# Two-layer GLA and short-conv encoder: attention stage cut into 512-token segments whose steps stand between projections

## The reference

```
q, k, v, r, gl = split(x @ w_in)             # 512 | 512 | 1024 | 1024 | 16
log_a = log_sigmoid(gl @ w_gate_up + b) / 16 # 512
cum = cumsum(log_a) inside each chunk of 64 tokens; tot = its last row
k_dec = k * exp(tot - cum)
S_c = exp(tot) * S_{c-1} + k_dec^T v         # per head, 128 x 256, 4 heads, 32 chunks
o = q @ S_c                                  # every token of chunk c reads the state after c
o = rmsnorm_per_head(o) * gn * silu(r)
x = x + o @ w_out
```

## Time and profile before

| | us |
|---|---|
| median of 3 runs | 1712.02 (1711.77 to 1791.83) |
| the profiled execution, device time | 1712.97 |
| its span on the slowest core (core 1) | 1711.7 |
| spans of the 8 cores | 1707.7 to 1711.7 |
| mean granted PE clock, all cores | 0.940 to 0.943 |

### The profile page before, as it was taken

How to read it: one execution, slowest core, us unless ns; L and a number is a source line. 1 busy time by engine, 2 the same in 40 slices (tenths; PEclk the granted TensorE clock), 3 DMA queues, 4 the chain that set the end, 5 groups by cost and what they waited for, 6 DMA issues and landing times.

```text
span 1711.7 us, 20982 instructions; the slowest of 8 cores (1707.7 to 1711.7 us)
## 1 busy us (share of the span) xinstructions
PE 1520.2 (89%) x7440; PEld 709.7 (41%) x7440; DVE 830.8 (49%) x1078; ACT 715.8 (42%) x1163; POOL 81.3 (5%) x123
## 2 busy tenths in 40 slices
PE   3996656995556699999999999999999999999998
PEld 1443223542223344444444454444544444444443
DVE  3013553105644455355545665556655544554557
ACT  5424435425446542044034564333654404412445
POOL 0010000010000000000000000000001000000000
PEclk9997677996777899999999999999999999999999
DMA  9562001561020033012322324333033202232204
GB/s 249 77 92 32 1 1 38 76 98 25 1 35 16 13 50 49 13 26 43 50 37 44 38 25 57 43 49 40 13 50 49 35 16 38 44 50 38 42 15 184
DMA packets 67557, 80.80 MB, mean 47 GB/s; under 512 B 4591, under 2 KB 54016, under 8 KB 67456
## 3 DMA queue, kind: packets, MB, share of 16 engines
q0 software_dynamic: 61840, 59.86, 25.5%
q1 hardware_dynamic: 5616, 19.62, 3.3%
HBM read 130.93 MB, written 8.39 MB: 81 GB/s over the span
## 4 chain that ended last, share of the span: by engine, by line
PE 83%; ACT 6%; DVE 5%; issue 3%; DMA 2%; DVEq 0%; ACTq 0%; POOL 0%; POOLq 0%; SPq 0%
PE PS L425 34%; PE PS L372 26%; PE PS L504 10%; PE PS L668 3%; PE PS L685 3%; DMA wring<-a_w_in 2%; PE PS L607 2%; PE PS L637 2%; DVE gl_ot_u L770 2%; ACT xtm L308 2%; DVE gl_s_u L730 1%; DVE gl_of_u L773 1%; PE PS L340 1%; ACT xn_shared_u L260 1%; PE PS L642 1%
## 5 line engine op out<-in xcount | busy, mean ns | idle before, releaser
L425 PE MATMUL PS<-xn_shared_u,wring 128*128 128x512 bf16 x2816 | 614.8, 381 | 5.1 <-ACT xn_shared_u L260 3.9
L425 PEld LDWEIGHTS PS<-xn_shared_u,wring 128*128 128x128 bf16 x2816 | 276.4, 98 | 340.0 <-issue 12.6
L372 PE MATMUL PS<-wring,ffn_h_u 128*128 128x512 bf16 x1408 | 306.8, 379 | 0.0
L379 DVE TENSOR_TENSOR X<-X,PS 128x512 f32<-128x512 f32 x256 | 174.2, 687 | 215.1 <-PE PS L372 212.6
L437 ACT ACTIVATE ffn_a_u<-PS,vecs_sb 128x1024 f32<-128x1024 f32 x88 | 98.1, 1114 | 274.3 <-PE PS L425 274.3
L372 PEld LDWEIGHTS PS<-wring,ffn_h_u 128*128 128x128 bf16 x1408 | 137.3, 98 | 163.3
L451 ACT ACTIVATE ffn_a_u<-ffn_a_u 128x1024 f32<-128x1024 f32 x88 | 93.0, 1057 | 228.3 <-DVE ffn_a_u L449 228.3
L504 PE MATMUL PS<-xn_shared_u,wring 128*128 128x512 bf16 x768 | 166.2, 379 | 1.2 <-ACT xn_shared_u L260 1.2
L452 DVE TENSOR_TENSOR ffn_h_u<-ffn_a_u,PS 128x1024 bf16<-128x1024 f32 x88 | 107.4, 1221 | 123.0 <-ACT ffn_a_u L451 117.7
L447 DVE SCALAR_TENSOR_TENSOR ffn_a_u<-ffn_g_u,vecs_sb,ffn_a_u 128x1024 f32<-128x1024 f32 x88 | 113.0, 1284 | 77.8 <-ACT ffn_g_u L445 73.2
L449 DVE SCALAR_TENSOR_TENSOR ffn_a_u<-ffn_g_u,vecs_sb,ffn_a_u 128x1024 f32<-128x1024 f32 x88 | 113.0, 1284 | 9.2
(11 more groups left out here) (83 smaller groups left out, 1092.8 us busy)
## 6 DMA issues: line engine op xcount, KB each, us to landing
wring<-f_w_up POOLq DMA_DIRECT2D x16, 1024.0 KB, 12.2
wring<-a_w_in POOLq DMA_DIRECT2D x12, 1024.0 KB, 14.4
wring<-f_w_down POOLq DMA_DIRECT2D x44, 256.0 KB, 9.5
X<-x SPq DMA_DIRECT2D x16, 512.0 KB, 15.8
out<-X SPq DMA_DIRECT2D x16, 512.0 KB, 2.7
wring<-f_w_up POOLq DMA_DIRECT2D x8, 768.0 KB, 12.0
wring<-b_w_in POOLq DMA_DIRECT2D x12, 512.0 KB, 10.3
wring<-a_w_out POOLq DMA_DIRECT2D x16, 256.0 KB, 6.9
```

The source lines that it names most:

```text
L372: ins = nc.tensor.matmul(self.PS[:, b, :], Y[:, k, yi * 128:(yi + 1) * 128], w[k].ap[:, n * 512:(n + 1) * 512], start=(k == 0), stop=(k == ...
L379: lambda: nc.vector.tensor_tensor(xs, xs, self.PS[:, b, :], ALU.add))
L425: ins = nc.tensor.matmul(self.PS[:, bank0 + t, :], w.ap[:, kc, jb * 128:(jb + 1) * 128], XN[:, kc, (hh * 2 + t) * 512:(hh * 2 + t + 1) * 512],
```

## The change

The attention stage has no halves and no barriers. After `gla_start` it is a loop over four segments of 512 tokens: `gla_project(sg)` (gate, q, r) and `gla_scan(sg)` (tile by tile k and v). The six weight blocks of `w_in` and `w_out` have places of their own in one arena (`at`, with `inherit` taking over the waits of what lay there before) and are loaded once. `w_out` comes as f32 by SP into the places of X tiles 8 to 15, DVE multiplies gn into it (`late_wo`) and writes bf16 `Wo`, and only then SP loads x tiles 8 to 15 (`late_x`). SP issues x tiles 0 to 3 first and waits for `Wk` before w_out and x tiles 4 to 7.

The scan works on tiles of two chunks. `g_update(g, hp)` makes two heads of both chunks in banks 4 and 5, `g_read(g)` writes both chunks' o into banks 6 and 7, where it stays: ACT squares it from there, `g_gated` multiplies it there by the rstd and then by silu(r). All other groups rotate over banks 0 to 3. Update, read-out, statistics, gating and output projection of tiles g-1 and g-2 stand between the projections of tile g; those of the segment's last tiles stand in the next `gla_project`, and after the last segment in the list `left`, which `ffn(0)` now pumps between its first matmuls together with the norms of tiles 8 to 15. Tiles 0 to 7 are normed for the FFN in the last segment's scan. The first four units (`hh` = 0) have banks 0 to 3 alone for their pairs.

`ffn`, `sconv` and the rest keep their operations; H, Y and XN are two tensors of 1024 tokens each.

```diff
-NXTM = 4
+NXTM = 3
...
-        self.gla()
-        with ExitStack() as eso:
...
+        self.gla_start()
+        for sg in range(T // SEG):
+            self.gla_project(sg)
+            self.gla_scan(sg)
+        left = self.gla_end()
+        self.load_gamma("b_norm")
+        self.ffn(0, left, lambda i: self.norm_tile("b_norm", i))
...
+    def gla_start(self):
...
+        for i in range(4):
+            self.sp.dma(self.X[:, i, :], xv[i], [], self.bX[i])
+            if i == 0:
+                self.load_gamma("a_norm")
+                self.sp.dma(self.consts[:], self.consts_d, [], [self.bconst])
+                self.sp.dma(self.vecs[:], self.vecs_d, [], [self.bconst])
...
+        self.pool.dma(self.WGU[0:17, :], self.a_wgu, [], [self.bWGU])
+        self.pool.dma(self.Wg[:], win[:, :, 3072:3088], [], [self.bWg])
+        self.pool.wait(self.bX[2][0].w)
+        self.pool.dma(self.Wq[:], win[:, :, 0:512], [], self.bWq)
+        for h in range(2):
+            self.pool.dma(self.Wr[:, h], win[:, :, 2048 + h * 512:2560 + h * 512], [], [self.bWr[h]])
+        self.pool.dma(self.Wk[:], win[:, :, 512:1024], [], self.bWk)
+        for h in range(2):
+            self.pool.dma(self.Wv[:, h], win[:, :, 1024 + h * 512:1536 + h * 512], [], [self.bWv[h]])
+        self.sp.wait(self.bWk[0].w)
+        for k in range(KC):
+            self.sp.dma(self.X[:, 8 + k, :], wout[k], [], self.bX[8 + k])
+        for i in range(4, 8):
+            self.sp.dma(self.X[:, i, :], xv[i], [], self.bX[i])
+        self.late_wo = [lambda k=k: self.dve.op(
+            self.bX[8 + k] + [self.bconst], [self.bWo[k]], lambda: nc.vector.tensor_scalar(
+                self.Wo[:, k, :], self.X[:, 8 + k, :], self.vcol("a_gn", k), None, ALU.mult))
+            for k in range(KC)]
+        self.late_x = lambda: [self.sp.dma(self.X[:, i, :], xv[i], [], self.bX[i]) for i in range(8, NTT)]
+        self.wo = [WBlock(self.Wo[:, k, :], [self.bWo[k]], None) for k in range(KC)]
+        self.singles = (0, 1, 2, 3)
+        for i in range(4):
+            self.norm_tile("a_norm", i)
+            self.turn(1)
+        self.turn()
...
+    def g_update(self, g, hp):
+        nc = self.nc
+        s = g % 2
+        def mmu():
+            ins = None
+            for h in (2 * hp, 2 * hp + 1):
+                for c in range(2):
+                    p = slice(c * 64, c * 64 + 64)
+                    ins = nc.tensor.matmul(self.PS[:, 4 + c, (h % 2) * 256:(h % 2 + 1) * 256],
+                                           self.KD[p, s, h * 128:(h + 1) * 128],
+                                           self.V[p, s, h * 256:(h + 1) * 256], start=True, stop=True)
+            return ins
+        self.pe.op([self.bKD[s], self.bV[s * 2 + hp]], [self.bPS[4], self.bPS[5]], mmu)
+        for c in range(2):
+            for h in (2 * hp, 2 * hp + 1):
+                self.dve.op([self.bS[(1 - c) * HEADS + h], self.bDEC[g], self.bPS[4 + c]], [self.bS[c * HEADS + h]],
+                            lambda: nc.vector.scalar_tensor_tensor(
+                                self.S[:, c, h, :], self.S[:, 1 - c, h, :], self.DEC[:, h, 2 * g + c:2 * g + c + 1],
+                                self.PS[:, 4 + c, (h % 2) * 256:(h % 2 + 1) * 256], ALU.mult, ALU.add))
+            hs = slice(2 * hp, 2 * hp + 2)
+            self.copy_on(self.act, self.SB[:, c, hs, :], self.S[:, c, hs, :],
+                         self.bS[c * HEADS + 2 * hp:c * HEADS + 2 * hp + 2], [self.bSB[c * 2 + hp]])
+    def g_read(self, g):
+        nc = self.nc
+        q = g // 4 % 2
+        i = g % 4
+        for c in range(2):
+            def mmo():
+                ins = None
+                for j in range(KC):
+                    h, hv = j // 2, j % 2
+                    ins = nc.tensor.matmul(self.PS[:, 6 + c, j * 64:(j + 1) * 64],
+                                           self.SB[:, c, h, hv * 128:(hv + 1) * 128],
+                                           self.QT[:, q, h, i * 128 + c * 64:i * 128 + c * 64 + 64], start=True, stop=True)
+                return ins
+            self.pe.op(self.bSB[c * 2:c * 2 + 2] + self.bQT[q * HEADS:(q + 1) * HEADS], [self.bPS[6 + c]], mmo)
+        self.act.op([self.bPS[6], self.bPS[7]], [self.bOF[g % 2]], lambda: nc.scalar.activation(
+            self.OF[:, g % 2].rearrange("p j (c t) -> p c j t", c=2),
+            self.PS[:, 6:8, :].rearrange("p c (j t) -> p c j t", t=64), AF.Square))
+    def g_stats(self, g):
+        nc = self.nc
+        b = self.bank()
+        osq = self.OF[:, g % 2].rearrange("p (h v) t -> p v h t", v=2)
+        def mmn():
+            nc.tensor.matmul(self.PS[:, b, :], self.onesV[:], osq[:, 0], start=True, stop=False)
+            return nc.tensor.matmul(self.PS[:, b, :], self.onesV[:], osq[:, 1], start=False, stop=True)
+        self.pe.op([self.bOF[g % 2], self.bconst], [self.bPS[b]], mmn)
+        self.rstd_from_psum(self.RS[:].rearrange("p h t -> p (h t)"), self.PS[:, b, :], [self.bPS[b]], self.bRS)
+    def g_gated(self, g):
+        nc = self.nc
+        i = g % 4
+        for c in range(2):
+            o = self.PS[:, 6 + c, :].rearrange("p (h v t) -> p h v t", h=HEADS, v=2)
+            rs = self.RS[:, :, c * 64:(c + 1) * 64].unsqueeze(2).broadcast_to([128, HEADS, 2, 64])
+            self.dve.op([self.bRS, self.bPS[6 + c]], [self.bPS[6 + c]], lambda: nc.vector.tensor_tensor(o, o, rs, ALU.mult))
+        self.dve.op([self.bPS[6], self.bPS[7]] + self.bSR, [self.bOF[g % 2]], lambda: nc.vector.tensor_tensor(
+            self.OF[:, g % 2].rearrange("p j (c t) -> p c j t", c=2),
+            self.PS[:, 6:8, :].rearrange("p c (j t) -> p c j t", t=64),
+            self.SR[:, :, i * 128:(i + 1) * 128].rearrange("p j (c t) -> p c j t", c=2), ALU.mult))
+    def gla_project(self, sg):
+        g = 4 * sg - 1
+        tail = g >= 0
+        norm = sg >= 1 and sg < 3
+        n0 = 4 * sg + 4
+        self.g_gate(sg)
+        if tail:
+            self.g_stats(g - 1)
+            self.g_update(g, 0)
+        if norm:
+            self.norm_tile("a_norm", n0)
+        self.g_softplus(4 * sg)
+        self.g_q(sg, 0)
+        if tail:
+            self.g_gated(g - 1)
+            self.g_update(g, 1)
+        if norm:
+            self.norm_tile("a_norm", n0 + 1)
+        self.g_q(sg, 1)
+        self.g_softplus(4 * sg + 1)
+        if tail:
+            self.g_out(g - 1)
+            self.g_read(g)
+        if norm:
+            self.norm_tile("a_norm", n0 + 2)
+            self.turn(2)
+        self.g_q(sg, 2)
+        self.g_decay(4 * sg)
+        if tail:
+            self.g_stats(g)
+        if norm:
+            self.norm_tile("a_norm", n0 + 3)
+            self.turn(2)
+        self.g_q(sg, 3)
+        if tail:
+            self.g_gated(g)
+        for j in range(KC):
+            self.g_r(sg, j)
+            if j == 2 and tail:
+                self.g_out(g)
+            if j in (4, 6):
+                self.turn(max(0, len(self.turns) - 1))
+    def gla_scan(self, sg):
+        for i in range(4):
+            g = 4 * sg + i
+            if sg == 0 and i >= 2:
+                self.norm_tile("a_norm", 2 * i)
+                self.norm_tile("a_norm", 2 * i + 1)
+            if sg == 3:
+                if i == 0:
+                    XNA, bXNA = self.at("xna", A_XNA, [128, KC, 1024], BF16, 8)
+                    self.XN[0] = XNA
+                    self.bXN = bXNA + self.bXN[8:]
+                self.norm_tile("f_norm0", 2 * i)
+            if 1 <= i < 3:
+                self.g_softplus(g + 1)
+            self.g_k(g)
+            if i >= 2:
+                self.g_stats(g - 2)
+            if i >= 1:
+                self.g_update(g - 1, 0)
+            self.g_v(g, 0)
+            if i >= 2:
+                self.g_gated(g - 2)
+            if sg == 3:
+                self.norm_tile("f_norm0", 2 * i + 1)
+                self.turn(1)
+            if i >= 1:
+                self.g_update(g - 1, 1)
+            self.g_v(g, 1)
+            if i < 3:
+                self.g_decay(g + 1)
+            if sg == 0 and i == 1:
+                for f in self.late_wo:
+                    f()
+                self.late_x()
+            if i >= 2:
+                self.g_out(g - 2)
+            if i >= 1:
+                self.g_read(g - 1)
+            if sg == 3:
+                self.turn()
+            elif sg == 0 and i >= 2:
+                self.turn()
+            if sg == 2 and i == 0:
+                self.load_gamma("f_norm0")
+    def gla_end(self):
+        g = NTT - 1
+        t, bufs = self.at("wring", A_RING, [128, NSLOT * 1024], BF16, 1)
+        rb = [Buf("ring%d" % i) for i in range(NSLOT)]
+        for i in range(4):
+            rb[i].inherit(self.bWq[0])
+            rb[4 + i].inherit(self.bWk[0])
+        self.ring = Ring(self.pool, NSLOT, t, rb)
+        self.pairs = (0, 1, 2, 3)
+        self.singles = (4, 5)
+        def n(i):
+            return lambda: self.norm_tile("f_norm0", i)
+        def t1():
```

(23 more changed lines are left out.)

746 lines of the change are left out of this document (308 added, 438 removed).

## The result

The changed kernel takes 1602.28 us (median of four runs, 1600.39 to 1620.1). Its ratio to the kernel before is 0.938, with a 95% interval of 0.927 to 0.950: faster. Forecast were 1586 and a range of 1540 to 1650. The profiled execution took 1600.39, its span was 1599.0. Executions in which the cores of one die ran over 1% longer than the other's at a lower clock are left out of the comparisons.

The account below looks back on a forecast made before the run. Before 574 us gaps and the half clock after them bound the kernel, later PE's matmuls. Start 122, segments 87, 87, 94 and hand-over 64 make 454; plus 1131 gives 1585 of span, 1586 us forecast, range 1540 to 1650.

Parts of the forecast that it names:

- PE's work of a segment, 76 us: Attention segment: matmul groups, decay, state updates, reads, statistics, gate-up and transposes sum to 76 us of PE work.
- Segments 87, 87, 94: Segments 1 to 3: walked times including waits; 87 us each for 1 and 2, 94 for 3, where ACT paces the scan.
- the lower bound: DVE's gating in its new PSUM form: 0.69 us for 512 elements and 1.22 for 1024, the upper bound being twice that.
- The start, 122: Segment 0: v of tile 0 waits for Wv to about 75 us, `late_wo` stops PE 6 us, stage ends at 122.
- My lower bound of 0.5: DVE's `late_wo` multiplies at the start: bounds 0.5 and 1.28 us each, 1.07 taken, 8.6 us for eight.
- If w_out and x were last instead of Wv: Start, other load order: v would start near 62 us and the stage would end near 108.
- The hand-over, 64: Attention's end to `hh` = 1, first four FFN units: 64 us; 52 if ACT hardly hinders, 80 if two banks do.
- 1131 from `hh` = 1 on: From `hh` = 1 to the end: instructions the same, three XTM tiles cost nothing, so 1131 us remain.
- PE hardly waits (1536): Rival: bank rotation covers ACT and DVE, segments 79, 79 and 86, start 108, FFN's 52; 1536 us, chance 20%.
- ACT and DVE set the pace (1668): Rival: casts waiting for DVE hold evacuations; segments 103, 103, 118, start 132, FFN 80; 1668 us, chance 22%.
- The clock that never rises: Rival: small gaps in dense stretches keep PE at 1.2 GHz, segments 155, 155, 165; 1847 us, slower, chance 2%.
- The sign for v: Start: first v projection at 65 to 76 us behind a DMA; v by 60 would mean the queue order was wrong.

Follow-up runs that it names:

- experiment 8: Changed kernel plus early w_out/`late_wo` start, gating before norms, state casts on GpSimd, norms in ACT's convolution wait: 1559.83 to 1573.87 us, ratio 0.907; casts on ScalarE: 1566.94.
- Experiment 3: Changed kernel, but SP waits for the last block of Wv instead of Wk before loading w_out and x tiles 4 to 7: 1587.6 us.
- experiment 4: Changed kernel, SP waiting for Wv, x before w_out, segment 0 norms and `late_wo` moved: 1581.14 us; w_out after x tile 4, `late_wo` in tile 1: 1581.08.
- experiment 7: Changed kernel's hand-over, three runs: attention and norms all before the FFN, 1608.11 us; first four units' Silu as Copy, hand-over 65.9; norms in ACT's convolution wait, 1590.87.
- Experiment 1: Changed kernel with each tile's update, read, statistics, gating and output projection straight after its v projection, not one or two tiles later: 1774.12 us.

## Why the prediction was right, and where its terms were off

The sign and the mechanism hold, and the size does: 1602 against 1586, of which the slowest core's distance from the median of the eight is 5.8. Part of the closeness is errors that cancel. Point by point:

- *PE's work of a segment, 76 us.* Right: with no stop over 0.5 us left inside it a segment takes 76.5 (experiment 8).
- *Segments 87, 87, 94.* Measured 83.5, 81.8, 92.6. The stop at the gating was there as walked, 3.8 us with 16 matmuls in 5.30 us behind it; the second one, 3 us ahead of tile g's output projection, wasn't: it starts at 164.22 us without a stop. My 41.5 for four scan tiles was 1 to 2 us too much as well. In segment 3 two errors cancel: the projections took 34.2 us where I had 38.5, the scan 58.7 where I had 55.5 (core 5):

```profile
333.30:392.00 58.70, 47.74 (x301) 23.82 (x299) 29.87 (x46) 42.62 (x79) 1.76 (x2) 0.91 0.14 19
```

The gating cost what the lower bound says, in rows:

```profile
L797 DVE TENSOR_TENSOR PS<-PS,gl_rs_u 128x512 f32<-128x512 f32 x32 | 20.7, 692 | 7.3 <-PE PS L655 5.3 <-ACT gl_rs_u L375 2.0
L798 DVE TENSOR_TENSOR gl_of_u<-PS,gl_sr_u 128x1024 bf16<-128x1024 f32 x16 | 19.6, 1225 | 1.9 <-DVE PS L797 0.7
L635 DVE TENSOR_SCALAR wo_u<-X,vecs_sb 128x1024 bf16<-128x1024 f32 x8 | 5.4, 748 | 0.0
```

- *The start, 122.* Measured 129.8, and this is the term that failed most. The second v group came at 75.6, where I had put 75, and for the reason given. From there I had 47 us and it took 54.2: one stop of 6 us in my walk, against 3.59, 5.15 and 2.30 (tile 1's update, tile 2's behind the two norms of tile 3, the first gate behind the transposes' copies), and half clock only in that v group, against 0.88 as the mean from 80 to 133.5 us. `late_wo` was priced too high on the other side: the eight took 5.4 us, 0.67 each, where I took 1.07. My lower bound of 0.5 was no bound: it was argued from a row half as long as the norm multiply's, and both have 1024 elements. The Trainium skill's page VectorE: DVE Perf Modes, section The perf-mode tier table, led to 0.65, and the trace agrees.
- *"If w_out and x were last instead of Wv ... the stage would end near 108."* Experiment 3 does that: v starts at 60.0, where I had 62, but the stage ends at 116.5; only with the order of DVE's and ACT's work changed too (experiment 4) is it 108.9.
- *The hand-over, 64.* Measured 69.7. That ScalarE's queue has a part in it is shown by experiment 7: another order of the same work on ACT and DVE gives 9.1 us back, six table loads less give 5.0. But it is no matter of ACT being full. I expected it to be over 75% busy in segment 3's scan and the four units; it was 73% and 62% (42.62 of 58.7, 43.25 of 70). It is the place in its queue, work behind a wait. My eight table loads were six. And I had no half clock there; 0.83 is what the row shows. The two shared banks, which I had priced only in the upper bound, hold the longest stop (5.95 us, in experiment 7); no run moves it.
- *1131 from `hh` = 1 on.* Measured 1135.8. I had said that the instructions from there on are the same and that three XTM tiles cost nothing. Behind that mark PE waits 8.3 us, against 2.5 before. 1.8 of the 4.8 us belong to the hand-over: ACT and DVE finish its last unit behind the mark and hold up PE there. With the hand-over in another order (experiments 1, 7 and 8) this stop is gone and the rest is 1134.0 or 1134.1 us:

```profile
471.86 8.36 PE L460 MATMUL PS<-xnb_u,wring_u 128*128 128x512 bf16 x38 [1.64 <-DVE ffn_h_u L490]
```

The largest of the waits stand at the start of the second FFN, in those runs too:

```profile
1139.67 5.30 PE L460 MATMUL PS<-xna_u,wring_u 128*128 128x512 bf16 x16 [3.17 <-ACT ffn_g_u L479]
...
1146.46 17.43 PE L460 MATMUL PS<-xna_u,wring_u 128*128 128x512 bf16 x80 [1.05 <-DVE ffn_h_u L490]
```

`pump` puts the last transposes of the short convolution's norms between the first groups of 16 there too, where before they came after a unit; their copies stand on ACT ahead of the reading of the gate banks. That this order is the cause is read from the rows; no run moved it alone.
- *The rivals.* PE hardly waits (1536): the scans came close, the ends didn't. ACT and DVE set the pace (1668): it holds only for the hand-over and, in part, segment 3's scan. The clock that never rises: segments ran at 0.94 to 0.98, and PE's stops of 0.4 to 0.8 us in the scan left it there. Experiment 1 shows the other side, 9.7 us of stops a tile: clock 0.78, and slower than before. That rival's condition was real, the change just stays clear of it.

Of the signs that I had named, `hh` = 1 at 440 to 485 us came (457.3 by the median), so did the clock from 125 to 390 (0.96) and PE's longest waits there, for the gating. ACT's share did not. The sign for v came in halves: Wv is loaded in two blocks, the second v group starts at 75.6 behind its DMA, as walked, but the first at 58.2 by the median, under the 60 that I had called a sign of a wrong queue order. It was the second block that the other queue held back, by 15.6 us (experiment 3); for the first PE waited 4.12 us on core 5.

So the sum came out 16 us low: start, hand-over and rest were 7.8, 5.7 and 4.8 us short, the segments gave 10.1 of that back, the slowest core added 5.8, and the median of the runs lies 1.9 above the profiled one.

## What to carry to other kernels

An engine that is 60% busy can still hold up the others: look for what stands behind a wait in its queue, and move work into the wait. If you move it to another engine instead, look at what else that engine's queue holds: on GpSimd the casts held up the issue of the next loads. Delay each step's consumer by one projection of independent work, and look whether the long stops are gone, since many of them are paid again in half clock. Of loads on two queues, issue first and alone what is needed first: here the queue with the small packets lost beside the other. And when an edit gains less than expected in a stage, look at that stage's stops for a new one before you call the theory wrong.

## What the runs showed of the hardware

- Both DMA queues active: about equal packets, not equal bytes (717 and 645 packets, 2.62 and 0.65 MB in 12 us); the hardware queue alone up to 419 GB/s.
- A DMA that GpSimd issues waits for the work ahead of it on GpSimd: with the casts there, the first FFN weights were issued at 376.85 instead of 316.75 us.
- GpSimd's cast of 128x512 f32 to bf16 took 0.65 us, as ACT's 0.62, and the state updates of VectorE beside it stayed at 1.64 to 1.66 us for four:

```profile
L759 POOL CAST gl_sb_u<-gl_s_u 128x512 bf16<-128x512 f32 x60 | 38.9, 649 | 317.2 <-DVE gl_s_u L753 312.6 <-POOL gl_sb_u L759 4.6
```

- The half clock stands behind stops, but not behind each, and which groups it slows moves with small shifts further up. The gate group took 3.50 us behind a stop of 2.30 in the changed kernel and 1.89 behind one of 2.35 in experiment 8. The update behind the 3.59 us ran its four matmuls in 0.39, and the v group after it took 2.97 where 1.90 is the full clock. A stage with no changed instruction moved by 2 us.
